# Second mixer, the part ahead of the heads: order of weight splits, rotation set-up, compression chunks, gates and query norm

## What is computed

```python
h = rms_norm_2(x, mix_norm_g[i])
(u, c_b, c_c, c_x, q, k_c, v_c, k_s, v_s, k_w, v_w, nsa_gates, mix_gates) = split_projection(h @ w_in[i])
y_ssm = s5_mixer(u, lam_re, lam_im, b_re, b_im, c_re, c_im, d, log_dt, w_glu)
y_conv = short_conv_mixer(c_x, c_b, c_c, conv_w, conv_w_out)
y_attn = nsa_mixer(q, k_c, v_c, k_s, v_s, k_w, v_w, nsa_gates, q_norm_g, k_norm_g, cmp_pe, cmp_w1, cmp_w2, w_o)
gates = sigmoid(mix_gates).reshape(bsz, seq, 3, D_MODEL)
mixed = gates[:, :, 0] * y_ssm + gates[:, :, 1] * y_conv + gates[:, :, 2] * y_attn
x = x + mixed @ w_out[i]
```

## Time and profile before

| | before |
|---|---|
| median of three runs | 1551.62 us |
| the profiled execution: time | 1547.13 us |
| the profiled execution: span | 1545.2 us |
| mean granted clock of TensorE | 0.977 of full |
| busy TensorE, VectorE, ScalarE, GpSimd | 96%, 74%, 50%, 9% |

### The profile page before, as it was taken

The page is one execution under the profiler, slowest core; times in us unless marked ns, Lnnn a source line. Parts: engine busy times, 40 slices in busy tenths (PEclk is TensorE's granted clock), DMA queues, the critical chain, the costliest instruction groups (busy, mean ns, idle before and its releaser), DMA issues.

```text
span 1545.2 us, 24303 instructions
## 1 busy us (share of the span) xinstructions
PE 1479.9 (96%) x8495; PEld 1283.3 (83%) x8495; DVE 1146.5 (74%) x1835; ACT 772.0 (50%) x1257; POOL 140.4 (9%) x139
## 2 busy tenths in 40 slices
PE   6999999899999999999899999979998999999999
PEld 5888888788888888879778888777987789888887
DVE  4877776777777777777767777866589967577776
ACT  5344366464444544346645434464588755354432
POOL 0000024100000000005110000101332310000000
PEclk9999999999999999999899999989898999999999
DMA  7665644446655566565344655535522245646652
GB/s 289 193 201 190 192 150 151 132 151 196 201 190 191 208 199 195 188 192 153 109 158 156 204 189 190 166 123 171 192 83 80 72 132 184 190 150 201 194 188 85
DMA packets 71072, 261.74 MB, mean 169 GB/s; under 512 B 8016, under 2 KB 8016, under 8 KB 70736
## 3 DMA queue, kind: packets, MB, share of 16 engines
q1 hardware_dynamic: 69696, 253.79, 50.8%
q10 hardware_dynamic: 1296, 6.85, 1.2%
HBM read 259.56 MB, written 1.05 MB: 169 GB/s over the span
## 4 chain that ended last, share of the span: by engine, by line
PE 87%; DVE 7%; ACT 4%; issue 2%; DMA 1%; POOL 0%; DVEq 0%; ACTq 0%
PE work L728 24%; PE work L729 12%; PE acc L466 8%; PE acc L468 8%; PE acc L467 8%; PE work L466 8%; PE work L467 7%; PE work L468 7%; DVE wlo L452 2%; PE work L1428 1%; PE acc L1457 1%; ACT whi L445 1%; DVE frac L1837 0%; PE work L1429 0%; ACT xboth L523 0%
## 5 line engine op out<-in xcount | busy, mean ns | idle before, releaser
L452 DVE TENSOR_TENSOR wlo<-raw,whi 128x1024 fp32r<-128x1024 f32 x460 | 548.2, 1219 | 206.3 <-ACT whi L445 203.0
L728 PE MATMUL work<-xboth,whi 128*128 128x512 f32 x1600 | 560.7, 393 | 0.0
L445 ACT ACTIVATE whi<-raw 128x1024 fp32r<-128x1024 f32 x480 | 474.9, 1039 | 48.9 <-PE work L468 35.4
L729 PE MATMUL work<-xboth,wlo 128*128 128x256 f32 x1600 | 445.3, 278 | 0.0
L728 PEld LDWEIGHTS work<-xboth,whi 128*128 128x128 f32 x1600 | 299.7, 187 | 68.6
L729 PEld LDWEIGHTS work<-xboth,wlo 128*128 128x128 f32 x1600 | 301.2, 188 | 4.3
L808 ACT ACTIVATE sg<-sg 128x256 f32<-128x256 f32 x100 | 41.8, 418 | 476.1 <-DVE sg L849 476.1
L468 PE MATMUL acc<-whi,hlo 128*128 128x512 f32 x440 | 173.8, 395 | 0.0
L467 PE MATMUL acc<-wlo,hhi 128*128 128x512 f32 x440 | 173.6, 395 | 0.0
L466 PE MATMUL acc<-whi,hhi 128*128 128x512 f32 x440 | 173.5, 394 | 0.0
L466 PE MATMUL work<-xboth,whi 128*128 128x256 f32 x488 | 144.4, 296 | 8.2 <-DVE wlo L452 8.2
(11 more groups left out here) (435 smaller groups left out, 2022.0 us busy)
## 6 DMA issues: line engine op xcount, KB each, us to landing
raw<-stream SPq DMA_DIRECT2D x480, 512.0 KB, 3.7
par<-pm ACTq DMA_DIRECT2D x2, 1644.5 KB, 7.3
pfa<-pf_a ACTq DMA_DIRECT2D x3, 516.0 KB, 3.6
pfb<-pf_b ACTq DMA_DIRECT2D x2, 516.0 KB, 8.0
x<-x_in SPq DMA_DIRECT2D x2, 512.0 KB, 5.8
out<-x SPq DMA_DIRECT2D x2, 512.0 KB, 2.6
par<-pm ACTq DMA_DIRECT2D x1, 820.0 KB, 4.3
pre<-pf_a ACTq DMA_DIRECT2D x1, 4.0 KB, 4.0
```

Of the source, the lines that this page charges most:

```text
L445: nc.scalar.activation(chunk(whi, place, c)[:, cols], chunk(raw, place, c)[:, cols], ACT.Copy).then_inc(hi_ready, 1)
L452: nc.vector.tensor_tensor(chunk(wlo, place, c)[:, cols], chunk(raw, place, c)[:, cols], chunk(whi, place, c)[:, cols].bitcast(F32), ALU.su ...
L728: nc.tensor.matmul(o[:, :], hi[:, k * P:(k + 1) * P], xboth[:, k, :], start=k == 0, stop=False)
L729: m = nc.tensor.matmul(o[:, 0:S], lo[:, k * P:(k + 1) * P], xhi[:, k, :], start=False, stop=k == KD - 1)
```

## The change

The order of chunks: the eight compression chunks (`W1_CHUNK`) no longer lie together ahead of the gate chunks but two by two, each pair followed by one gate chunk. TensorE runs half of hid0, e0, the other half, e1, half of hid1, e2, the rest, e3, and then hidt, e4, cmp, e5, the transposes, kct, e6, the compressed scores and e7. The banks' order follows. ScalarE starts with the evacuations of q and the splits of 6 to 9; the rotation set-up is laid between the later projections (exponentials ahead of u0, sines behind it, turns of table 0 ahead of u2, table 0 behind the compression's blocks, turns of table 1 behind kv0). VectorE's list follows, and norms the query ahead of the keys, right after chunk 15; GpSimd's power is split into a part for q (16 columns), ahead of the coefficient chain, and one for k (8 columns), behind it. Gates e4 to e7 are parked in `pfa` in place of a part of `xn`, e8 to e11 the other way round. The parameter load moves to before the last FFN of the first block.

```diff
-D_Q, ..., D_U3, D_W1, D_EARLY = 0, 4, 8, 9, 12, 16, 17, 25
+D_Q, ..., D_U3, D_MIXED = 0, 4, 8, 9, 12, 16, 17
+W1_CHUNK = [D_MIXED + c for c in (0, 1, 3, 4, 6, 7, 9, 10)]
+E_CHUNK = [D_MIXED + c for c in (2, 5, 8, 11, 12, 13, 14, 15)] + [D_ROUNDS + c for c in (15, 16, 17, 19, 20, 21, 22, 23, 24)]
-"u3", "hid0", "hid1", "e0", "e1", "hidt0", "hidt1", "e2", "cmp0", "cmp1", "e3", "qt00", "qt01", "qt10", "qt11", "kt0", "kt1", "e4", "kct", "e5", "e6", "cs0", "cs1", "e7"
+"u3", "hid0", "e0", "e1", "hid1", "e2", "e3", "hidt0", "hidt1", "e4", "cmp0", "cmp1", "e5", "qt00", "qt01", "qt10", "qt11", "kt0", "kt1", "kct", "e6", "cs0", "cs1", "e7"
# TensorE
+            for w in range(2):
+                for half in range(2):
+                    compress(w, half)
+                    early(2 * w + half)
# ScalarE
             split_hi(act, place, [4, 5])
-            act.wait_ge(par_loaded, 3 * 16)
-            s5a.inc(nc.scalar.activation(s5p[:, 0, :], par[:, PN["ldt"]], ACT.Exp))
...
-            turns(0)
-            tables(0)
-            turns(1)
             job2.wait(act, JOB2["q0"])
             copy("q0", xn[:, 0, 0:512], bank2("q0"))
...
             split_hi(act, place, [14])
+            act.wait_ge(par_loaded, 3 * 16)
+            s5a.inc(nc.scalar.activation(s5p[:, 0, :], par[:, PN["ldt"]], ACT.Exp))
+            s5v.wait(act, 2)
+            s5a.inc(nc.scalar.activation(s5p[:, 3, :], s5p[:, 1, :], ACT.Exp))
+            inputs(0)
+            s5v.wait(act, 3)
+            s5a.inc(... ACT.Sin, scale=TWO_PI)
+            s5a.inc(... ACT.Sin, scale=TWO_PI / 2)
+            inputs(1)
+            act.wait_ge(consts2, 8)
+            turns(0)
+            inputs(2)
             for w in range(2):
                 xc32.wait(act, w + 1)
                 xcs.inc(nc.scalar.activation(xchi[:, w], xc[:, w], ACT.Copy))
+            masks.inc(...)
+            tables(0)
             copy("kv0", xn[:, 0, 512:], bank2("kv0"))
+            turns(1)
             projected(D_KV + 3)
...
+            for w in range(2):
+                split_hi(act, place, [c + 6 for c in W1_CHUNK[4 * w:4 * w + 2]])
+                early(2 * w)
+                projected(W1_CHUNK[4 * w + 3])
+                emptied(f"hid{w}", ... ACT.Gelu_apprx_tanh)
+                split_hi(act, place, [c + 6 for c in W1_CHUNK[4 * w + 2:4 * w + 4]])
+                early(2 * w + 1)
# VectorE, in the new order
             split_lo(dve, place, [4, 5])
+            split_lo(dve, place, range(6, 10))
+            ... squared(t, slice(0, 512), 8, 0) for both t; mean(slice(0, 8))
+            split_lo(dve, place, range(10, 14))
+            split_lo(dve, place, [14])
+            dve.wait_ge(par_loaded, (LAYERS + 1) * 16)
             s5a.wait(dve, 1)
...
+            split_lo(dve, place, [15])
+            nrm.wait(dve, 1)
+            ... q3 scaled by qk_rstd and by q_g for both t
+            split_lo(dve, place, [16])
             s5a.wait(dve, 4)
...          (the nineteen coefficient steps)
             ... xc additions
+            dve.wait_ge(consts2, 8)
+            fraction(0)
+            split_lo(dve, place, [17])
             ... xclo
+            squared(0, slice(512, 768), 4, 8)
+            fraction(1)
+            squared(1, slice(512, 768), 4, 8)
+            mean(slice(8, 12))
             split_lo(dve, place, range(18, 22))
             split_lo(dve, place, [22])
             ... y5lo
+            split_lo(dve, place, range(23, 26))
+            nrm.wait(dve, 2)
             ... k3 for both t
+            split_lo(dve, place, range(26, 29))
+            split_lo(dve, place, range(29, E_CHUNK[4] + 7))
# GpSimd
+            mean_pow(rstds[:, :, 0:8], means[:, :, 0:8], 8)
             coef_ready.wait(pool, 1)
...          (the nine coefficient instructions)
+            s5m.wait(pool, 2)
+            mean_pow(rstds[:, :, 8:12], means[:, :, 8:12], 4)
# ScalarE's block, layer LAYERS - 1
+                    act.dma_start(par[:, 0:NPN], pm2).then_inc(par_loaded, 16)
                 ffn_act(act, l * 2 + 1, l * 3 + 2, f2, following)
...
-            act.dma_start(par[:, 0:NPN], pm2).then_inc(par_loaded, 16)
-            act.wait_ge(consts2, 8)
```

More of the change, by code:

```diff
@@ L161 @@
 ROUNDS = 16
-BANKED2 = (["q0", "q1"] + [f"kvc{i}" for i in range(4)] + ["ng", "u0", "u1", "u2", "kv0", "kv1", "u3", "hid0", "hid1", "e0", "e1",
-           "hidt0", "hidt1", "e2", "cmp0", "cmp1", "e3", "qt00", "qt01", "qt10", "qt11", "kt0", "kt1", "e4", "kct", "e5", "e6", "cs0", "cs1", "e7"])
+BANKED2 = (["q0", "q1"] + [f"kvc{i}" for i in range(4)] + ["ng", "u0", "u1", "u2", "kv0", "kv1", "u3", "hid0", "e0", "e1", "hid1", "e2",
+           "e3", "hidt0", "hidt1", "e4", "cmp0", "cmp1", "e5", "qt00", "qt01", "qt10", "qt11", "kt0", "kt1", "kct", "e6", "cs0", "cs1", "e7"])
 BANK2 = {name: k % 4 for k, name in enumerate(BANKED2)}
 BY_DVE2 = ["cmp1", "cs0", "cs1", "bu0"]
-BY_ACT2 = [name for name in BANKED2 if name not in BY_DVE2]
+BY_ACT2 = BANKED2[:BANKED2.index("hid0")] + ["e0", "hid0", "e1", "e2", "hid1"]
+BY_ACT2 += [name for name in BANKED2[BANKED2.index("e3"):] if name not in BY_DVE2]
 JOBS2 = ["q0", "kv0"] + [name for name in BANKED2[BANKED2.index("hidt0"):] if name[0] != "e"]
@@ L1358, in mix2_pe, with early, compress @@
             channels("u3", D_U3)
[L1360 to L1364, removed]
+            def early(*js):
+                for j in js:
+                    channels(f"e{j}", E_CHUNK[j])
+            def compress(w, half):
+                if half == 0:
+                    begin2(pe, f"hid{w}")
+                    xc_ready.wait(pe, w + 1)
+                for j in range(8 * half, 8 * half + 8):
+                    c = W1_CHUNK[4 * w + j // 4]
                     pe.wait_ge(lo_ready, place.count(c))
@@ L1400, in mix2_pe @@
                     done(name, m)
+            qn_ready.wait(pe, 2 * T)
             for t in range(T):
@@ L1821, in mix2_dve, with fraction, squared, mean @@
             split_lo(dve, place, [4, 5])
+            split_lo(dve, place, range(6, 10))
+            def fraction(g):
+                for i in range(2):
+                    tab_k.wait(dve, 4 * g + 4)
+                    step(stt(out=frac[:, i, :], in0=tokens_f[:, :], scalar=s5p[:, 2, 2 * g + i:2 * g + i + 1], in1=frac[:, i, :], op0=ALU.mult, op1=ALU.subtract))
+                frac_ready.inc(ts(frac[:, :, :], frac[:, :, :], 0.5, -0.5, ALU.min, ALU.max))
+            means = qk_ms[:, :].rearrange("p (t n) -> p t n", t=T)
+            def squared(t, cols, heads, at):
+                n = cols.stop - cols.start
+                step(tt(sq[:, t, 0:n], xn[:, t, cols], xn[:, t, cols], ALU.mult))
+                step(nc.vector.tensor_reduce(qk_ms[:, t * 12 + at:t * 12 + at + heads], sq[:, t, 0:n].rearrange("p (h n) -> p h n", h=heads), AX.X, ALU.add))
+            def mean(cols):
+                s5m.inc(ts(means[:, :, cols], means[:, :, cols], 1.0 / HD, EPS, ALU.mult, ALU.add))
+            for t in range(T):
+                evac2.wait(dve, BY_ACT2.index(f"q{t}") + 1)
+                squared(t, slice(0, 512), 8, 0)
+            mean(slice(0, 8))
+            split_lo(dve, place, range(10, 14))
+            split_lo(dve, place, [14])
+            dve.wait_ge(par_loaded, (LAYERS + 1) * 16)
             s5a.wait(dve, 1)
```

98 lines of the change are left out of this document (32 added, 66 removed).

## The result

The changed kernel takes 1538.56 us (median of 4 runs, 1536.16 to 1539.82), the kernel before on the same chip 1551.26 us (4 runs, 1549.57 to 1552.19): ratio 0.9917, 95% interval 0.9900 to 0.9935, a gain of 12.9 us by that ratio, with 10.1 to 15.5 as its bounds. The forecast was 13.5 us and 1538.1. The time was met; the sum behind it was not, as the rows show: one term, 1.5 us, measured 6.2 with the low clock behind it, and the gain was larger than forecast in two other places.

The account below looks back on a forecast made before the run. The order of work, not its amount, was taken to make TensorE wait and drop to half clock. Gains of 15.3 us less 1.8 paid gave 13.5, so 1551.62 would become 1538.1 us; range 1533.5 to 1543 for 8 in 10.

Parts of the forecast that it names:

- Part 1: Splits of chunks 6 to 9 first: the first gap, before kvc2, goes (8.2 us), with its low clock (2.0 us).
- Part 2: Rotation set-up spread behind later projections: chunk 15 in time, a new wait of 0.2 us for chunk 18 in the plain sum.
- Part 3: GpSimd's coefficient chain beside VectorE ahead of chunk 18: six instructions slowed, new wait 0.2 to 3.2 us, taken as 1.5.
- Part 4: Gates between compression chunks: the second gap, at chunk 23, goes (3.65 us), with the low clock behind it (1.5 us).
- Parts 5 and 6: Early query norm and one block fewer behind the transposes: cost 0.3 us (0 to 1.0); earlier parameter load: nothing, at most 0.4.
- B: Half-clock stretch in the narrow gate projection and the block behind it, 3.1 us lost; forecast to stay.
- D: Half-clock stretch behind the 32 tiny matmuls of the compressed scores, some 2.1 us lost; no gain counted.
- Luck with B and D: Rival, chance 0.10: these low clocks depend on what comes before; without the first 1535.0 us, without both 1532.9.
- Contention: Rival, chance 0.15: GpSimd's chain costs VectorE all 3.2 us, bank wait 1.0, another clock fall 1.5: 1542.0 us.
- The transposes: Rival, chance 0.10: the clock falls on the 24 transposes and what follows them, costing 3.1 us: 1541.2 us.

Follow-up runs that it names:

- e1: The changed kernel run again with no edit, as the level for other runs: 1538.91 us, ratio 0.9914 to the kernel before.
- e2: The changed kernel with GpSimd's nine-instruction coefficient chain left out, one memset in its place: 1533.39 us, ratio 0.9878 to the kernel before.
- e3: The changed kernel with GpSimd's coefficient chain moved behind its two other powers, nothing left out: 1532.38 us, ratio 0.9869 to the kernel before.
- e11: The changed kernel with the chain behind both powers and the rotation set-up back ahead of the query copies and splits 6 to 9: 1541.70 us, ratio 0.9940.
- e9: The kernel of e3 run again, as the level for two later runs: 1531.85 us, ratio 0.9874 to the kernel before.
- e6: The changed kernel with its eight compression chunks together again and four gates behind them: 1538.42 us, ratio 0.9926 to the kernel before.
- e10: The changed kernel with the chain behind both powers and the eight compression chunks together again: 1532.04 us, ratio 0.9876 to the kernel before.
- e12: The kernel of e10 with query and key norms ahead of the low halves of chunks 23 to 25: 1537.73 us, ratio 0.9904 to the kernel before.
- e8: The changed kernel with the parameter load put back behind the mixer's entry: 1535.57 us, ratio 0.9912 to the kernel before.
- e5: The changed kernel with the rotation set-up put back ahead of the query copies and splits 6 to 9: 1542.18 us, ratio 0.9951.
- e7: The changed kernel with the query norm put back beside the key norm, behind chunk 25: 1537.40 us, ratio 0.9919 to the kernel before.
- e4: The changed kernel with GpSimd's coefficient chain moved behind the key's power only: 1536.91 us, ratio 0.9903 to the kernel before.

## Why the prediction came out right, and where it was wrong

**Part 1 (splits first): right.** Chunk 6 was split from 1014.61 (forecast 1015 to 1016), there is no idle time ahead of kvc2 and no low clock there. q0 to hid0 takes 55.7 to 56.2 us in the changed kernel, e1, e2 and e3, where it was 66.6 before. e11 gives the price: 9.9 us, against 8.2 + 2.0.

**Part 2 (set-up spread): right in the plain sum.** Chunk 15 was in time. Chunk 18 came, with no chain beside, at the moment it was wanted: e2 and e3 show a pause of 0.3 us, the forecast had 0.2.

**Part 3 (the chain beside VectorE): right in its mechanism and mis-sized.** Forecast 1.5 us (called the middle of 0.2 to 3.2, which is 1.7), at most 3.2; measured 4.65 and a low clock of 1.5 behind it, 6.2 in all; e3 and e9 put it at 6.5 us or so by the medians. Three things in this step failed. The price of one instruction, 0.5 us, came from a low half, which takes 1.22 us alone; here most instructions take 0.4 to 0.5 alone and lose 0.7 to 1.0 (the two first, the block additions, 0.4). The count was six, of two operands each; nine lay beside the chain, one of them, the clamp of the fractions, with a single operand. And the sum stopped short of the clock: a gap of 4.65 us was followed by 16 matmuls at half clock, as the gap of 3.65 was in the earlier trace rows.

The sentence of the Trainium skill that stood beside this step, SBUF — State Buffer, section "SBUF: two separate sides", has the port held by one engine for a whole instruction. For the chain this case's rows agree: nine instructions beside nine, VectorE's 1.25 us apart on average, GpSimd's mostly 1.1 to 1.35 long. An estimate by that rule charges each of the nine one GpSimd instruction of some 1.2 us less its own length, and the low half nothing: 6.2 us, and not 6 x 0.5; measured are 6.9, since the low half lost 0.85 too. The row of 1.72 us that I preferred was of a long instruction, the one kind that hides the rule.

For GpSimd's powers the rows do not agree. In the kernel before, this one runs beside the low halves of chunks 18 to 22, which take 5.80 us for five, 1.16 each, as long as without it:

```profile
1065.87 5.08 POOL L1775 TENSOR_TENSOR qk_rstd<-qk_ms,halves 128x24 f32<-128x24 f32 x1 [59.68 <-DVE qk_ms L1884]
```

In e3 the power of 8 columns (2.56 us from 1055.69) costs the four low halves beside it nothing either (4.63 us from 1055.52). So a GpSimd instruction's length is not its price; those of the chain handle 512 columns, the powers 8 to 24. Whether it's the size or the operation that matters was not tried.

**Part 4 (interleaving): the gain right, its cause wrong.** The second gap and its low clock went. The prediction put that down to the gate blocks between the compression chunks. e6 and e10 undo these and nothing comes back; e12 moves two norms on VectorE and the gap of 3.9 us does. The prediction named the norms as what VectorE did between 1065.70 and 1077.63, and then credited another part of the diff. The first and the last row of the norms in the kernel before:

```profile
1072.76 0.68 DVE L1894 TENSOR_TENSOR xn<-xn,qk_rstd 128x512 f32<-128x512 f32 x1
...
1077.10 0.62 DVE L1899 TENSOR_TENSOR xn<-xn,par 128x128 f32<-128x128 f32 x2
```


**Parts 5 and 6: right.** The transposes wait 0.2 + 0.2 us (forecast 0.3); the parameter load costs nothing (e8). That nothing is won by it holds for the new order only: with the set-up first, the load behind the mixer's entry held the set-up up for 0.4 us of the first gap (see e5).

**Low clock B and D, which were to stay.** B stayed nearly in sum. In and behind the gate projection the changed kernel's trace loses 1.5 us where the prediction reckoned 3.1 for that stretch, but the first matmuls of q0 lose 1.7 in place of the 0.6 of the kernel before. In e1, the same kernel, it is as before (3.1 and 0.5), and q0 to hid0 is 56.1 there, 10.5 less than before; in the changed kernel's trace 10.9, where 8.2 + 2.0 was forecast. D shrank: from the compressed scores to the head scores it is 9.8 us before (1108.41 to 1118.19) and 8.2 in the changed kernel and in e1, e2, e3 and e9, a gain of 1.55 that no term of the sum has; only the rival "Luck with B and D" has one of that kind. The two other kernels with the query norm late, e7 and e12, have 9.8 again, but e5, with the norm early, has 9.5; so the norm alone doesn't settle it, and the cause stays open.

**The sum again, for the profiled pair**, by the three pieces of the stage: q0 to hid0, forecast 10.2, measured 10.9; hid0 to the compressed scores, forecast 3.65 + 1.5 - 1.5 - 0.3 = 3.35 gained, measured 1.1 lost, almost all of it part 3; from there on to the head scores, forecast nothing, measured 1.55 gained. Together 11.3 where 13.5 stood (10.6 in e1, whose stage is 107.6). The medians differ by more, 12.7 and 13.2 us, since the profiled execution of the kernel before lay 4.1 us below the median of its kind and that of the changed kernel 2.4; at which places the others lose those microseconds no trace here shows. That the median of 1538.56 lies 0.5 us from the forecast is thus luck as well as reason. Of the rivals, "Contention" had the mechanism of part 3 (a long wait, then another fall of the clock), which measured more than the rival gave; its bank wait of 1.0 did not come. Its 1542.0 did not come about, because the two terms above and that difference of the medians lay on the other side. The transposes (1091.03 to 1094.15) did not lower the clock: it is full from 1096 to 1100 behind them, and no wait there is over 0.2.

**A better version.** The kernel of e3 and e9, which moves two powers ahead of the chain, takes 1531.85 and 1532.38 us, ratios of 0.9874 and 0.9869 to the kernel before, 6.5 us below the changed kernel (e1, beside e3 on the same chip).

## What to carry over

When a step is moved so that GpSimd and VectorE work side by side on data in SBUF, look in a trace for how long VectorE's small instructions take beside just these GpSimd instructions. Beside instructions like those of this chain (128x512 fp32, 1.1 us), charge each small one the full length of its neighbour; beside a power of 8 to 24 columns nothing was lost here. Put GpSimd's long chains where VectorE has slack, or behind what others wait for. Name for each gap the instructions that stood ahead of the late one, and look for where the diff moves exactly these. A gap that goes with the change is no proof for the part that one had in mind; undoing that part alone settles it.

## What the hardware showed that I had not expected

An instruction of 0.4 us on VectorE takes 1.3 us beside a chain of 1.1 us instructions on GpSimd (four of them together 1.42 alone and 5.30 in e4), while one of 1.22 takes 2.07 or less (1.49 on average in e4): the loss does not grow with the instruction's own length. A power of 24 columns on GpSimd, 5.08 us long, costs VectorE nothing. The clamp of the fractions, which reads a single operand, suffers the same: 0.43 to 1.16 us. GpSimd pays too, most beside VectorE's low half of 2.07: a sum of two tiles takes 2.16 us there, where the same kind of sum took 1.35 ahead of it. And the low clock behind a gap has no fixed length: after 4.65 us of idle 16 matmuls, after 4.66 us in another execution of the same kernel 20, after 3.86 us 28.
